# Keys' squares in rounded parts, summed by rounded matmuls, with the first query product ahead of the sums

## The chip, the cores and the metric

The kernel runs on one core of a Trainium2 chip. The metric is the device time of one execution in microseconds (us). The engines of the core work side by side, each through its own list of instructions in order, and meet at semaphores: PE (TensorE, matmuls), ACT (ScalarE), DVE (VectorE), POOL (GpSimd) and SP (which only issues transfers here).

## What is computed

Two layers of a decoder block on 528 tokens (16 meta tokens and 512 others), 1024 channels wide. Each layer normalizes its input, multiplies it by one wide matrix and feeds three mixers: a gated linear recurrence, a short gated convolution and an attention of 8 heads with low-rank queries and keys. The mixers' gated outputs are projected, merged and added back. The part that matters here is how the keys are normalized:

```python
def rms_norm(x, g):
    xf = x.astype(jnp.float32)
    y = xf * lax.rsqrt(jnp.mean(xf * xf, axis=-1, keepdims=True) + EPS)
    return (y * g.astype(jnp.float32)).astype(x.dtype)

def mla(...):
    q = (rms_norm(c_q, cq_g) @ w_uq).reshape(b_, t_, MLA_HEADS, QK_HEAD)
    ckv = rms_norm(c_kv, ckv_g)
    k_nope = (ckv @ w_uk).reshape(b_, t_, MLA_HEADS, QK_NOPE)
    v = (ckv @ w_uv).reshape(b_, t_, MLA_HEADS, V_HEAD)
    k_r = jnp.broadcast_to(k_rope[:, :, None, :], (b_, t_, MLA_HEADS, QK_ROPE))
    k = jnp.concatenate([k_nope, k_r], axis=-1)
    q = rms_norm(q, qn_g)
    k = rms_norm(k, kn_g)        # the sum of squares over a head's 192 channels
    ...
```

## The kernel before

Everything lies with channels on the 128 partitions and the 528 tokens along the free dimension. A product of two float32 matrices is made of three matmuls on rounded operands (type fp32r in the profile): each operand is split into an upper part, rounded to fp32r, and a lower part, the rest. Upper times upper, lower times upper and upper times lower are accumulated in PSUM (`product`, L499, its matmuls at L507). 528 columns make two matmuls of 264. POOL splits each 512 KB weight unit as it arrives (`split`, L411 to L420); ACT and DVE split activations: ACT writes the upper part, DVE subtracts it from the whole (`lo_part`, L1093).

Attention works through pairs of heads, four pairs in each of two layers, so eight turns of one loop (`Fori` over `PAIRS`; PE's loop starts at L647, ACT's at L878, DVE's at L1242, POOL's at L450). A turn on PE goes in this order: values for four token tiles (`va`, L660), keys of two heads (`kn0`, `kn1`, L507), values of the fifth token tile (`vb`, L660), the sums of the keys' squares (`sum_k0`, `sum_k1`, L557), the queries of two heads (`qn0`, `qn1`), their rotated part (`qr`), then "fill" steps. A fill step is six matmuls of an ordinary projection of the layer, which belongs to the convolution mixer and to the gates; its products have the names `c0`, `x0`, `g0`, `b0` and so on. Fill steps stand wherever PE would otherwise wait: five of them, then the queries' sums of squares by token (`stat_q`, L541, one column each, in three portions with a fill step behind each portion), 16 more, and then ten rounds of scores (L572, L575), fill, and transposes of the probabilities (L590). `b0` is the first fill product behind the first scores.

The sum of squares over the channels is a sum over partitions. `spread_sum` (L554) makes it with a matmul whose stationary operand is a 128x128 tile of ones, which leaves the sum in every partition. Squares and ones are float32 there, so this is a float32 matmul; the profile has two records for each one.

The other engines in a turn, in their orders. ACT: upper part of `va` (L883); for each key head its square (L888) and the key times its gain (L890), which frees the key's PSUM slot; upper part of `vb` (L893); two square roots (L897), which wait for DVE's sums; then square and upper part of each query (L903, L904) and of `qr` (L907, L909). DVE: lower part of `va` (L1245) and of `vb` (L1251), squares of keys plus the squares of the shared rotated part (L1258, twice), a reciprocal (L1264) and the lower part of a query (L1270) for each head, then the keys' normalization and lower parts and those of the rotated parts (L1279 to L1316), a small reciprocal (L1319), and the convolution's input (L1384), which frees the PSUM slot that `b0` takes. POOL: weight units, and between units 3 and 4 the addition of the queries' squares (L467), for which `stat_q` waits.

PSUM is used as four slots of two banks each. `TILES` (L80) lists which product takes which slot and which semaphore it signals; a product waits until the slot's last reader has let it go. Waits are counts computed from these tables.

Of the kernel before, what the change touches and what calls it, by code (L numbers as in the profile page):

```python
# [28 lines left out]
P = 128  # L29
# [56 lines left out]
            ("sum_k0", 0, "att_mm"), ("sum_k1", 1, "att_mm"), ("qn0", 2, "att_mm"), ("qn1", 3, "unit_used"),  # L86
# [9 lines left out]
for _s in ("MR", "MS"):  # L96
# [16 lines left out]
    "k_squared": ("ATT", 2), "v_hi": ("ATT", 2), "k_sum": ("ATT", 1), "k_rms": ("ATT", 2), "q_summed": ("ATT", 2), "k_rinv": ("ATT", 2), "k_full": ("ATT", 2), "kr_scaled": ("ATT", 2),  # L113
# [35 lines left out]
def build(nc, xt, w_units, w_pair, params, hparams, consts, rope, stream):  # L149
    with ExitStack() as ctx:  # L150
# [64 lines left out]
        ones = sb("ones", [P, P])  # L215
        lane_consts = sb("lane_consts", [P, 2 + 2 * NTOK])
# [179 lines left out]
        def _(pool):  # L396
            pool.memset(ones[:], 1.0).then_inc(sem("made"), 1)
            pool.memset(eps, EPS).then_inc(sem("made"), 1)
# [88 lines left out]
        def _(pe):  # L487
# [123 lines left out]
            for l in range(DEPTH):  # L611
# [33 lines left out]
                with nc.Fori(0, PAIRS, engines=bass.OrderedEngineSet([pe.engine]), head_slot={pe.engine: 0}) as p:  # L645
# [26 lines left out]
                    for h in range(2):  # L672
                        out = free("ATT", l, p, f"sum_k{h}")
                        pe.wait_ge(*at("k_squared", l, p, h + 1))
                        spread_sum(out, ct[h]).then_inc(sem("att_mm"), 1)

                    pe.wait_ge(*was_read("CQ", l, 0, "q2"))
                    hi, lo = unit_ready("ATT", l, p, 1)
                    for h in range(2):
                        out = free("ATT", l, p, f"qn{h}")  # L680
                        product(out, lambda k: hi(3 * h + k), lambda k: lo(3 * h + k), tiles(cq_hi), tiles(cq_lo),
                                KQ).then_inc(sem("unit_used" if h else "att_mm"), 1)
                    out = free("ATT", l, p, "qr")
# [91 lines left out]
        def _(act):  # L775
# [50 lines left out]
            for l in range(DEPTH):  # L826
# [51 lines left out]
                with act.Fori(0, PAIRS) as p:  # L878
# [7 lines left out]
                    for h in range(2):  # L886
                        act.wait_ge(*ready("ATT", l, p, f"kn{h}"))
                        act.activation(halves(ct[h][:]), slot(slot_of("ATT", f"kn{h}")), ACT.Square).then_inc(  # L888
                            sem("k_squared"), 1)
                        act.activation(halves(ct[2 + h][:]), slot(slot_of("ATT", f"kn{h}")), ACT.Identity, bias=zero,  # L890
                                       scale=hparam(l, KN_G)).then_inc(freed("ATT", f"kn{h}"), 1)
# [22 lines left out]
                    for h in range(2):  # L914
                        act.wait_ge(*at("k_full", l, p, h + 1))
                        act.activation(kn_hi[:, h, :], ct[2 + h][:], ACT.Copy).then_inc(sem("k_hi"), 1)
# [175 lines left out]
        def _(dve):  # L1092
# [39 lines left out]
            for l in range(DEPTH):  # L1132
# [109 lines left out]
                with dve.Fori(0, PAIRS) as p:  # L1242
# [10 lines left out]

                    for h in range(2):
# [402 lines left out]
```

## Time and profile before

| | us |
|---|---|
| runs of the kernel (three) | 1724.68, 1726.32, 6525.27 |
| median | 1726.32 |
| the profiled execution, device time | 1722.76 |
| its span in the trace | 1721.0 |
| PE busy | 1700.5 (99%) |
| POOL busy | 1204.6 (70%) |
| DVE busy | 887.7 (52%) |
| ACT busy | 485.6 (28%) |

Times in the trace are microseconds from the start of the span. A row of the timeline has start, duration, engine, line and operation, output and inputs, and how many instructions are merged in it (x2). A matmul's duration is from its start to its modelled end; the next one starts long before that end, so the cost of a matmul in a row of many is the distance between starts. Brackets at the end of a row give the idle time ahead of it and what ended it. In a table of windows each row has the stretch, its length, the busy time of PE, PEld, DVE, ACT and POOL with their instructions, then PEclk, the granted clock of TensorE (1.00 for full speed), the busy share of the DMA engines and GB/s.

### The profile page before, as it was taken

To read this page: it belongs to the slowest core of one execution; us is meant where nothing else is said; L and a number is where in the kernel's file an instruction comes from. 1 tells how busy PE (TensorE), PEld (TensorE's weight loads), DVE (VectorE), ACT (ScalarE), POOL (GpSimd) and SP (SyncE) were. 2 spreads that over 40 slices of the span, in tenths; PEclk is the share of its full clock that TensorE was granted. 3 is DMA by queue.
4 is the path that set the end of the run, shared out by engine and by line. 5 is a ranking of instruction groups with operands and counts; after the bars stand their busy time and mean duration, and the time that the engine had idled before them with its cause. 6 is when DMAs were issued, how large, how long until landed. Compare 5 with 4: busy or idle time off the path is not lost.

```text
span 1721.0 us, 32258 instructions
## 1 busy us (share of the span) xinstructions
PE 1700.5 (99%) x11956; PEld 1593.7 (93%) x11956; DVE 887.7 (52%) x1281; ACT 485.6 (28%) x867; POOL 1204.6 (70%) x1365
## 2 busy tenths in 40 slices
PE   7999999999999999999999999999999999999999
PEld 7999999999999999999999998989898888888887
DVE  7966658485545452212349657584856455322221
ACT  5523233342313331101134333333323223311110
POOL 7764748385688777777766748483857898777773
PEclk9999999999999999999999999999999999999999
DMA  4421212122222223222432312121222322322233
GB/s 159 138 97 62 92 60 92 66 85 86 93 91 90 88 104 118 85 93 90 160 118 75 109 56 98 60 92 66 92 86 88 108 85 85 136 97 97 87 122 112
DMA packets 49407, 164.21 MB, mean 95 GB/s; under 512 B 6048, under 2 KB 7456, under 8 KB 49056
## 3 DMA queue, kind: packets, MB, share of 16 engines
q1 hardware_dynamic: 41328, 146.56, 25.4%
q10 hardware_dynamic: 8032, 17.03, 3.0%
q8 instruction: 29, 0.48, 0.1%
q14 instruction: 18, 0.15, 0.0%
HBM read 152.21 MB, written 10.81 MB: 95 GB/s over the span
## 4 chain that ended last, share of the span: by engine, by line
PE 96%; POOL 1%; DVE 1%; DMA 1%; ACT 0%; issue 0%; ACTq 0%; POOLq 0%; DVEq 0%
PE slots L507 84%; PE slots L572 4%; PE slots L605 3%; PE slots L660 2%; POOL early L467 1%; PE slots L590 1%; PE slots L541 1%; PE slots L557 1%; DMA residual_or_merged<-xt 1%; DVE spare L1115 0%; ACT early L907 0%; PE slots L575 0%; DVE branch_lo L1106 0%; PE slots L550 0%; DVE cq_lo L1150 0%
## 5 line engine op out<-in xcount | busy, mean ns | idle before, releaser
L419 POOL TENSOR_TENSOR w_lo<-w_raw,w_hi 128x256 fp32r<-128x256 f32 x1004 | 839.6, 866 | 20.9
L414 POOL TENSOR_SCALAR w_hi<-w_raw 128x1024 fp32r<-128x1024 f32 x251 | 290.5, 1157 | 345.9 <-PE slots L507 337.1
L507 PE MATMUL slots<-h_hi,w_hi 128*128 128x264 f32 (+1 forms) x2112 | 523.5, 312 | 0.0
L507 PE MATMUL slots<-h_lo,w_hi 128*128 128x264 f32 (+1 forms) x2112 | 517.1, 309 | 0.0
L507 PE MATMUL slots<-h_hi,w_lo 128*128 128x264 f32 (+1 forms) x2112 | 515.9, 308 | 0.0
L507 PEld LDWEIGHTS slots<-h_hi,w_hi 128*128 128x128 f32 x2112 | 343.8, 189 | 19.3
L507 PEld LDWEIGHTS slots<-h_hi,w_lo 128*128 128x128 f32 x2112 | 343.1, 189 | 19.1
L507 PEld LDWEIGHTS slots<-h_lo,w_hi 128*128 128x128 f32 x2112 | 343.2, 189 | 17.8
L507 PE MATMUL slots<-branch_hi,w_hi 128*128 128x264 f32 (+1 forms) x576 | 143.7, 313 | 9.9 <-DVE branch_lo L1106 9.2
L507 PE MATMUL slots<-branch_lo,w_hi 128*128 128x264 f32 (+1 forms) x576 | 142.4, 311 | 0.0
L507 PE MATMUL slots<-branch_hi,w_lo 128*128 128x264 f32 (+1 forms) x576 | 142.0, 310 | 0.0
L1463 DVE SCALAR_TENSOR_TENSOR gated<-gate_tanh,slots 128x528 f32<-128x528 f32 (+1 forms) x32 | 22.3, 696 | 179.4 <-PE slots L507 179.4
L507 PEld LDWEIGHTS slots<-branch_hi,w_hi 128*128 128x128 f32 x576 | 94.6, 190 | 16.6 <-issue 10.6
L1017 ACT ACTIVATE gate_tanh<-slots,channel_params 128x528 f32<-128x528 f32 (+1 forms) x48 | 33.4, 695 | 269.1 <-PE slots L507 269.0
L507 PEld LDWEIGHTS slots<-branch_lo,w_hi 128*128 128x128 f32 x576 | 94.0, 189 | 5.6
L507 PEld LDWEIGHTS slots<-branch_hi,w_lo 128*128 128x128 f32 x576 | 94.0, 189 | 5.5
L952 ACT ACTIVATE residual_or_merged<-slots,r_bias,q_sc 106x106 f32<-106x106 f32 (+4 forms) x80 | 49.4, 617 | 165.1 <-DVE r_bias L1337 165.1
L1359 DVE TENSOR_TENSOR pt_lo<-slots,pt_hi 106x106 fp32r<-106x106 f32 (+4 forms) x80 | 37.0, 463 | 65.3 <-ACT pt_hi L965 38.9
L1094 DVE TENSOR_TENSOR branch_lo<-sc_back,branch_hi x16 | 17.4, 1124 | 92.0 <-ACT branch_hi L1074 92.0
L965 ACT ACTIVATE pt_hi<-slots 106x106 fp32r<-106x106 f32 (+1 forms) x64 | 25.1, 393 | 125.7 <-PE slots L590 125.7
L414 POOL TENSOR_SCALAR w_rope_hi<-w_rope_raw 128x384 fp32r<-128x384 f32 x8 | 4.1, 513 | 74.3 <-PE slots L605 74.3
L1264 DVE RECIPROCAL early<-early 128x528 f32<-128x528 f32 x16 | 55.2, 3448 | 1.0
(234 smaller groups left out, 2828.1 us busy)
## 6 DMA issues: line engine op xcount, KB each, us to landing
w_raw<-w_units SPq DMA_DIRECT2D x251, 512.0 KB, 3.3
stream<-sc_acc ACTq DMA_DIRECT2D x16, 264.0 KB, 2.1
sc_back<-stream SPq DMA_DIRECT2D x2, 2112.0 KB, 8.0
x_old<-stream SPq DMA_DIRECT2D x16, 264.0 KB, 4.6
stream<-residual_or_merged ACTq DMA_DIRECT2D x16, 264.0 KB, 2.5
ab_raw<-w_units SPq DMA_DIRECT2D x8, 512.0 KB, 4.3
residual_or_merged<-xt ACTq DMA_DIRECT2D x4, 528.0 KB, 7.9
stream<-xt ACTq DMA_DIRECT2D x1, 2112.0 KB, 11.7
```

Source lines behind the costliest of these rows:

```text
L414: pool.tensor_scalar(hi, raw, 1.0, 1.0, ALU.mult, ALU.mult).then_inc(sem("hi_part"), 1)
L419: op = pool.tensor_tensor(lo[:, cols], raw[:, cols], hi[:, cols].bitcast(F32), ALU.subtract)
L507: mm = pe.matmul(out[:, a_, 0:t1 - t0], w(k), x(k)[:, t0:t1], start=(n == 0), stop=(n == 3 * ks - 1))
L572: mm = pe.matmul(bank[:, 0:k1 - k0], q[:, q0:q0 + nq], k[:, k0:k1], start=(m == 0), stop=(m == 4 and not masked))
L605: mm = pe.matmul(out[:, a_, q0 - a_ * HALF:q1 - a_ * HALF], v[0:nk, j, h * VHEAD:(h + 1) * VHEAD], pt[0:nk, j * PT_STEP + q0:j * PT_STEP + ...
L660: mm = pe.matmul(out[0:nt_, t % 4 // 2, (t % 2) * 256:(t % 2) * 256 + 256], x[:, k, t0:t0 + nt_], w[0][:, cols], start=(k == 0 and n == 0) ...
L952: act.activation(dst, src, ACT.Exp, bias=r_bias[0:nq, n:n + 1], scale=q_sc[0:nq, n:n + 1], accum_out=r_sum[0:nq, n:n + 1]).then_inc(sem("p ...
L965: act.activation(dst[:, :, 0:nq], src[:, :, 0:nq], ACT.Copy).then_inc(sem("turned_hi"), 1)
L1017: act.activation(kept_halves(l, g_t[n][:]), kept_slot(l, n), ACT.Tanh, bias=param(l, which, i * 2 + n), scale=0.5).then_inc(freed(stage, f ...
L1264: dve.reciprocal(ct[4 + h][:], ct[4 + h][:]).then_inc(sem("k_rinv"), 1)
L1359: dve.tensor_tensor(lo[:, :, 0:nq], src[:, :, 0:nq], hi[:, :, 0:nq].bitcast(F32), ALU.subtract).then_inc(done, 1)
L1463: dve.scalar_tensor_tensor(out, kept_halves(l, g_t[n][:]), 1.0, kept_slot(l, 2 + n), ALU.add, ALU.mult).then_inc(freed(stage, f"{y}{n}"), 1)
```

## The change

The squares of each key head are now kept as two rounded parts. ACT computes the square twice, into float32 (`ct[h]`) and rounded into `kn_hi[:, h]`; DVE subtracts the second from the first into `kn_lo[:, h]`, by its `lo_part`. PE sums each head with four fp32r matmuls (two halves, each with the upper and the lower part) against a rounded tile of ones, `ones_r`, which POOL makes once at the start. `kn_hi` and `kn_lo` hold the normalized key later in the same turn; ACT's write of it waits for the second sum. The first query product `qn0` now stands ahead of the two sums.

```diff
-            ("sum_k0", 0, "att_mm"), ("sum_k1", 1, "att_mm"), ("qn0", 2, "att_mm"), ("qn1", 3, "unit_used"),
+            ("qn0", 2, "att_mm"), ("sum_k0", 0, "att_mm"), ("sum_k1", 1, "att_mm"), ("qn1", 3, "unit_used"),
...
+        ones_r = sb("ones_r", [P, P], F32R)
...
+            pool.wait_ge(sem("made"), 1)
+            pool.tensor_scalar(ones_r[:], ones[:], 1.0, 1.0, ALU.mult, ALU.mult).then_inc(sem("ones_rounded"), 1)
...
-                    for h in range(2):
-                        out = free("ATT", l, p, f"sum_k{h}")
-                        pe.wait_ge(*at("k_squared", l, p, h + 1))
-                        spread_sum(out, ct[h]).then_inc(sem("att_mm"), 1)
-
                     pe.wait_ge(*was_read("CQ", l, 0, "q2"))
                     hi, lo = unit_ready("ATT", l, p, 1)
-                    for h in range(2):
+
+                    def queries(h):
+
                         out = free("ATT", l, p, f"qn{h}")
                         product(out, lambda k: hi(3 * h + k), lambda k: lo(3 * h + k), tiles(cq_hi), tiles(cq_lo),
                                 KQ).then_inc(sem("unit_used" if h else "att_mm"), 1)
+
+                    queries(0)
+                    for h in range(2):
+                        out = free("ATT", l, p, f"sum_k{h}")
+                        pe.wait_ge(*at("k_sq_lo", l, p, h + 1))
+                        for a_ in range(2):
+                            cols = slice(a_ * HALF, (a_ + 1) * HALF)
+                            for n, squares in enumerate((kn_hi, kn_lo)):
+                                mm = pe.matmul(out[:, a_, 0:HALF], ones_r[:], squares[:, h, cols], start=(n == 0),
+                                               stop=(n == 1))
+                        mm.then_inc(sem("att_mm"), 1)
+                    queries(1)
...
+                        act.activation(halves(kn_hi[:, h, :]), slot(slot_of("ATT", f"kn{h}")), ACT.Square).then_inc(
+                            sem("k_sq_hi"), 1)
...
+                        if h == 0:
+                            act.wait_ge(*ready("ATT", l, p, "sum_k1"))
                         act.activation(kn_hi[:, h, :], ct[2 + h][:], ACT.Copy).then_inc(sem("k_hi"), 1)
...
+                    for h in range(2):
+                        dve.wait_ge(*at("k_squared", l, p, h + 1))
+                        dve.wait_ge(*at("k_sq_hi", l, p, h + 1))
+                        lo_part(kn_lo[:, h, :], ct[h][:], kn_hi[:, h, :], "k_sq_lo")
```

On PE, between the fifth token tile's values and the second query product, before (`cq_hi` and `cq_lo` are the latent queries; the first group of `cq` rows is `qn0`, the row that waits for `slot_free3` begins `qn1`):

```order
L660 MATMUL slots<-w_hi,kv_lo 104x256
L513 REGISTER_ALU
L674 REGISTER_ALU [waits slot_free0]
L557 MATMUL slots<-early,ones 128x264 [waits k_squared]
L557 MATMUL slots<-early,ones 128x264
L513 REGISTER_ALU
L674 REGISTER_ALU [waits slot_free1]
L557 MATMUL slots<-early,ones 128x264 [waits k_squared]
L557 MATMUL slots<-early,ones 128x264
L492 REGISTER_ALU [waits slot_free0]
L513 REGISTER_ALU [waits unit_split]
L507 MATMUL slots<-cq_hi,w_hi 128x264 [waits slot_free2]
```

And the same place now, from the last rows of `qn0` on:

```order
L510 MATMUL slots<-cq_hi,w_lo 128x264 x2
L516 REGISTER_ALU
L687 REGISTER_ALU [waits slot_free0]
L691 MATMUL slots<-kn_hi,ones_r 128x264 [waits k_sq_lo]
L691 MATMUL slots<-kn_lo,ones_r 128x264
L691 MATMUL slots<-kn_hi,ones_r 128x264
L691 MATMUL slots<-kn_lo,ones_r 128x264
L516 REGISTER_ALU
L687 REGISTER_ALU [waits slot_free1]
L691 MATMUL slots<-kn_hi,ones_r 128x264 [waits k_sq_lo]
...
L516 REGISTER_ALU
L510 MATMUL slots<-cq_hi,w_hi 128x264 [waits slot_free3]
```

The sums now stand between the two query products, with twice the matmuls, and wait for DVE (`k_sq_lo`) and no longer for ACT alone (`k_squared`).

On DVE, from the lower parts of the values to the first reciprocal, now (before, the row with `kn_lo` was not there and the rest was the same):

```order
L1261 TENSOR_TENSOR v_lo<-slots,v_hi 106x1024 [waits v_hi]
L1266 REGISTER_ALU
L1267 TENSOR_TENSOR v_lo<-slots,v_hi 104x256 [waits v_hi]
L1110 TENSOR_TENSOR kn_lo<-early,kn_hi 128x528 [waits k_sq_hi,k_squared] x2
L1275 ISA
L1278 TENSOR_TENSOR early<-slots,residual_or_merged 128x528 [waits slot_free3,att_mm]
L1275 REGISTER_ALU
L1278 TENSOR_TENSOR early<-slots,residual_or_merged 128x528 [waits att_mm]
L1284 RECIPROCAL early<-early 128x528 [waits k_rms]
```

The two subtractions stand behind the lower part of `vb`, which needs ACT's copy of it, and ahead of everything that DVE does with the sums.

## Rows read from the trace of the kernel before

**Rows 1.** The page: the span, and busy time of the engines.
```profile
span 1721.0 us, 32258 instructions
...
PE 1700.5 (99%) x11956; PEld 1593.7 (93%) x11956; DVE 887.7 (52%) x1281; ACT 485.6 (28%) x867; POOL 1204.6 (70%) x1365
```

**Rows 2.** PE's waits: who waited for whom, total us, times, longest.
```profile
PE slots L507 <- DVE branch_lo L1106: 9.2, 4, 8.6
PE slots L541 <- POOL early L467: 4.5, 8, 0.6
```

**Rows 3.** PE's timeline, third pair of layer 0: float32 sums, then queries.
```profile
253.17 2.06 PE L557 MATMUL slots<-early,ones 128*128 128x264 f32 x8
254.87 0.60 PE L507 MATMUL slots<-cq_hi,w_hi 128*128 128x264 f32 x2
255.31 0.41 PE L507 MATMUL slots<-cq_lo,w_hi 128*128 128x264 f32 x2
...
257.27 0.41 PE L507 MATMUL slots<-cq_hi,w_hi 128*128 128x264 f32 x2
```

**Rows 4.** ACT's timeline, same pair: squares, gained keys, `vb`, square roots.
```profile
251.20 0.61 ACT L888 ACTIVATE early<-slots 128x528 f32<-128x528 f32 x1 [0.35 <-PE slots L507]
251.71 0.79 ACT L890 ACTIVATE early<-slots,lane_consts,head_params 128x528 f32<-128x528 f32 x1
...
253.16 0.79 ACT L890 ACTIVATE early<-slots,lane_consts,head_params 128x528 f32<-128x528 f32 x1
253.84 0.38 ACT L893 ACTIVATE v_hi<-slots 104x256 fp32r<-104x256 f32 x1
255.33 1.42 ACT L897 ACTIVATE early<-early,lane_consts 128x528 f32<-128x528 f32 x2 [1.11 <-DVE early L1258]
```

**Rows 5.** DVE's timeline, same pair.
```profile
254.26 0.42 DVE L1251 TENSOR_TENSOR v_lo<-slots,v_hi 104x256 fp32r<-104x256 f32 x1 [2.15 <-ACT v_hi L893]
254.60 1.38 DVE L1258 TENSOR_TENSOR early<-slots,residual_or_merged 128x528 f32<-128x528 f32 x2
256.10 3.45 DVE L1264 RECIPROCAL early<-early 128x528 f32<-128x528 f32 x1
...
263.41 0.67 DVE L1270 SCALAR_TENSOR_TENSOR qn_lo<-slots,head_params,qn_hi 128x528 fp32r<-128x528 f32 x1
```

**Rows 6.** POOL's timeline: same pair, and the first pair of layer 0.
```profile
254.22 2.12 POOL L419 TENSOR_TENSOR w_lo<-w_raw,w_hi 128x256 fp32r<-128x256 f32 x3
...
67.84 1.06 POOL L414 TENSOR_SCALAR w_hi<-w_raw 128x1024 fp32r<-128x1024 f32 x1 [4.42 <-DMA w_raw<-w_units]
```

**Rows 7.** Instructions of `lo_part` on DVE: ns min/median/max, first and last start.
```profile
L1094 DVE TENSOR_TENSOR kn_lo<-early,kn_hi x16: 1235/1257/1276, 82.9 to 1226.5; 128x528 fp32r<-128x528 f32 x16
...
L1094 DVE TENSOR_TENSOR kv_lo<-early,kv_hi x4: 696/697/700, 51.1 to 917.8; 128x528 fp32r<-128x528 f32 x4
```

**Rows 8.** Same pair, the queries' sums: POOL's addition, then PE.
```profile
262.62 3.25 POOL L467 TENSOR_TENSOR early<-early 64x528 f32<-64x528 f32 x2 [5.59 <-ACT early L907]
...
265.05 0.40 PE L507 MATMUL slots<-h_hi,w_lo 128*128 128x264 f32 x2
266.02 0.88 PE L541 MATMUL slots<-ones,early 128*106 128x1 f32 x8 [0.56 <-POOL early L467]
```

**Rows 9.** `b0`: DVE's last release and PE's first `b0` matmul, layer 0, then layer 1.
```profile
280.59 0.71 DVE L1384 TENSOR_TENSOR sc_pad<-slots,sc_c 128x528 f32<-128x528 f32 x1 [0.22 <-DVE q_sc L1319]
...
282.44 0.47 PE L507 MATMUL slots<-h_hi,w_hi 128*128 128x264 f32 x2
...
1049.03 0.71 DVE L1384 TENSOR_TENSOR sc_pad<-slots,sc_c 128x528 f32<-128x528 f32 x1 [0.22 <-DVE q_sc L1319]
...
1050.57 0.45 PE L507 MATMUL slots<-h_hi,w_hi 128*128 128x512 f32 x1
```

**Rows 10.** Windows after `stat_q`, pairs two and three: busy us, PE first; granted clock third from last.
```profile
172.10:178.90 6.80, 6.80 (x34) 6.80 (x33) 6.70 (x11) 3.45 (x8) 6.72 (x6) 0.50 0.22 77
...
268.50:275.30 6.80, 6.80 (x59) 6.80 (x58) 6.70 (x11) 4.42 (x8) 6.72 (x6) 1.00 0.23 77
```

More of the change, by code:

```diff
@@ L112 @@
     "rope_split": ("ATT", 1), "att_mm": ("ATT", 10),
-    "k_squared": ("ATT", 2), "v_hi": ("ATT", 2), "k_sum": ("ATT", 1), "k_rms": ("ATT", 2), "q_summed": ("ATT", 2), "k_rinv": ("ATT", 2), "k_full": ("ATT", 2), "kr_scaled": ("ATT", 2),
+    "k_squared": ("ATT", 2), "k_sq_hi": ("ATT", 2), "k_sq_lo": ("ATT", 2), "v_hi": ("ATT", 2), "k_sum": ("ATT", 1), "k_rms": ("ATT", 2), "q_summed": ("ATT", 2), "k_rinv": ("ATT", 2), "k_full": ("ATT", 2), "kr_scaled": ("ATT", 2),
     "k_hi": ("ATT", 2), "k_lo": ("ATT", 2), "krp_hi": ("ATT", 2), "krp_lo": ("ATT", 2),
```

## The prediction

> **What bounds the kernel now.** I read the page first: PE is busy for 1700.5 of 1721.0 us [rows 1]. Then PE's waits: besides one wait of 8.6 us at the start the only one that comes back in every turn of the attention loop is that of `stat_q` for POOL, 8 times and 4.5 us in all [rows 2]. So PE sets the time; a matmul taken off it is worth its distance to the next start, and a wait put on it costs as long as it is. What decides here is how much air the other engines have behind PE in one stretch, from the keys to the first scores. For that I read the timelines of all engines in the third pair of layer 0 [rows 3 to 9]; the other pairs agree with it within some hundredths from one start to the next, the first pair of each layer aside, where DVE and ACT are later.
>
> **What the sums cost and will cost.** The four float32 matmuls (eight records) run from 253.17 to 254.87, 1.70 us, and the query behind them loses 0.19 more (254.87 to 255.31 for two matmuls, where two otherwise take 0.24) [rows 3]. fp32r matmuls of 264 columns stand (257.27 - 255.31)/16 = 0.122 us apart [rows 3], so eight take 0.98. The swap gives 1.89 - 0.98 = 0.91 us a turn, 7.3 us in eight turns. That is all there is to gain.
>
> **What the sums will wait for.** Times are those of the third pair [rows 3 to 5]. PE is through with `vb` at 253.17 and does `qn0` at once (its slot, that of `va`, is free by then): 18 x 0.122 = 2.20, to 255.37.
> - ACT does one more square for each key. A square costs 0.51 from start to start (251.20 to 251.71), a gained key 0.68 (253.16 to 253.84) [rows 4]. The row is now 251.20, 251.71, 252.22 for the first head, 252.90, 253.41, 253.92 for the second, and `vb` at 254.60 and not 253.84. It ends at 254.98.
> - DVE's lower part of `vb` starts at 255.02 and is through at 255.44; the next instruction may start 0.08 before that (254.26 + 0.42 against 254.60) [rows 5]. Then the two new subtractions. The trace has such instructions at two prices: 0.70 us where POOL rests (`kv_lo`) and 1.26 where POOL splits weights (`kn_lo`, same shape) [rows 7]. In this stretch POOL is splitting a unit until 256.34 at least [rows 6], and slowed by DVE it goes on longer. So I take the higher price: ends at 256.6 and 257.8. The lower one would give 256.1 and 256.7. In the first pair of layer 0 POOL waits for a transfer from 63.4 to 67.8 [rows 6], and the lower price holds.
> - A wait costs PE 0.15 from the release to the first matmul (265.87 to 266.02) [rows 8]. First sum from 256.75, 1.4 us after PE was free; second from 257.97, 0.7 us after the first; `qn1` from 258.46. Before it began at 257.27 [rows 3]. PE is 1.2 us late: the 0.9 gained is gone, and 2.1 of waiting came.
>
> The Trainium skill, page "SBUF — State Buffer", section "Who interferes with whom", speaks against the new work: a VectorE instruction with two inputs in SBUF contends with a GpSimd instruction that reads SBUF, and whichever is first keeps the shared ports to its end. By that rule each subtraction would wait for the rest of a POOL piece of 0.7 us (2.12 for three [rows 6]) and take 0.7 to 1.4, which puts the second one's end between 256.7 and 258.1; the trace agrees, with 1.26 against 0.70 [rows 7].
>
> **What is late next.** DVE adds the second sum once it has landed, at about 258.65 to 259.35; then the reciprocals (3.45) follow. The first was at 256.10, bound by ACT's root [rows 4, 5], and is now at 259.35 at the latest. This chain of reciprocal, query, reciprocal, query has no air in it (256.10 to 264.08), so all behind it on DVE shifts by D = 3.25; if the first subtraction has the ports partly for itself, D is 2.9. I take D = 3.1. In the first pair of layer 0, by the same steps with 0.70 for a subtraction, D = 2.3.
> - `stat_q` takes the slot of `qn1`, which DVE frees at the end of that chain: before at 264.08, two microseconds ahead of PE; now at 267.2, so PE starts at 267.3 and not 266.02 [rows 5, 8]. POOL's addition is no longer what ends the wait: ACT is at `qr` when PE delivers it, 1.2 late. So PE is 1.3 late here, of which 1.2 was already there.
> - All through the keys' normalization to L1384 DVE has no pause but one of 0.22, so its release of `b0`'s slot shifts by D too. Before it came at 281.30 and PE, adding 0.15, wanted it at 282.44: air of 0.99. In layer 1 (pieces of 512 columns, a quicker fill) it is 1050.57 - 0.15 - 1049.74 = 0.68 [rows 9]. So PE's delay at `b0` is D less the air: 2.1 us a turn in layer 0 and 2.4 in layer 1. The 1.3 from `stat_q` are within that, not on top.
> - Behind `b0` rounds of scores, softmax and transposes hang on PE's own start of the scores, so they shift as one.
>
> Other parts cost nothing: `ones_r` is made once at the start, where POOL goes on to wait for the first weights (if that cover were gone: one instruction of 128 columns, and L414 does 1024 in 1.06 us [rows 6], so 0.1 to 0.3 us with its wait); ACT's wait for the second sum lies a dozen microseconds before its write.
>
> **The sum.** First pair of layer 0: 2.3 - 0.99 = 1.3. Three further pairs of layer 0: 2.1 each, four of layer 1: 2.4 each. Together 1.3 + 6.3 + 9.6 = 17.2 us. The gain of 7.3 is already in it, since it is worked out from starts.
>
> **The clock.** In pair two of layer 0 the granted clock fell to 0.50 (1.2 GHz) right behind `stat_q` and stayed for 6.8 us. 34 matmuls ran in this window against 59 in the same stretch of the next pair [rows 10]: 6.8 x 25/59 = 2.9 us lost. It came after the wait of 0.56 and the matmuls of one column, and seven other pairs with the same rows kept 2.4 GHz. Now the wait there is about 1.0 us and a new one of 2.1 us in two pieces stands before. So I expect it in more pairs. Part of a loss at `stat_q` falls into the air that PE now has at `b0` (2.1 - 1.3 = 0.8 in layer 0, 1.1 in layer 1), so a fall costs about 2 there, and one at the sums next to nothing. Before had one at 2.9; I take one and a half to two of them now at 2, +3 to 4 against -2.9, in all 0.5 more. Bounds: none now, -3; one in each pair, 16 - 3 = +13.
>
> The profiled execution took 1722.76, so the sum is 1722.76 + 17.2 + 0.5 = 1740.5. The two undisturbed runs, 1724.68 and 1726.32, lie 2 to 3.5 above it, so a median should come out near **1742 us**, 0.9% slower.
>
> **Rivals.**
> - *The clock falls in most pairs.* Speaking for it: each turn has two stretches poorer in matmuls than the one that brought it down. Against: seven of eight kept the clock. 17 + 13 gives 1755. Chance 0.15.
> - *The shift is small.* The subtractions take 0.70 in each pair, D = 2.3 and delays of 1.3 and 1.6: 4 x 1.3 + 4 x 1.6 = 12, less the 2.9 if pair two keeps the clock, 9: 1734. For it: they start just as POOL ends a unit. Against: POOL still has two of four pieces to do. Chance 0.15.
> - *Faster: the sums find their parts ready.* One mechanism: `qn0`'s 2.2 us cover ACT's and DVE's new work. Then only the swap counts, 7.3 us, and 1718 comes out. It decides at one point: the second lower part must be there by 255.7, and by my steps it is 2 us later, since it queues behind `vb` on two engines. For it speaks only that POOL and PE stay as they are. Chance 0.07.
> - *The change does not do what it says,* the fp32r sums cost as much as float32 ones. The waits hide it: a second sum of 0.85 in place of 0.49 gives 0.4 more in D, 1745. Inside my range, not counted by itself.
>
> **Chances and range.** My forecast 0.63, the rivals 0.15, 0.15 and 0.07. The forecast's own range, from D between 2.9 and 3.25 and the clock between none and three falls, is 1736 to 1748. For eight in ten I leave the faster case out below and the last of the clock case above: 1729 to 1756. A measurement of this kernel can tell about 2%, 35 us, from no change. Faster by that would need five times what the swap gives: 0.01. Slower by that needs a fall of the clock in each pair and more: 0.05. Within 2%: 0.94.
>
> **What would show it.** In the changed profile: eight records of sums a turn 0.12 us apart within a head; PE waiting 1 to 1.5 us for DVE's `kn_lo` ahead of the first and 0.5 to 0.7 ahead of the second; `kn_lo` of squares at 1.2 us except in the first pair; `stat_q` released by DVE's L1290 in place of POOL; a wait ahead of the first scores or of `b0`, ended by DVE, summing to about 2 us a turn with that at `stat_q`; stretches of half clock in the attention pairs. I am wrong if PE shows no wait at the sums, if DVE's chain up to the scores is shorter than before, or if a wait stands in the score rounds.

## The result and the profile after

| | before | after |
|---|---|---|
| median, us | 1725.5 | 1743.45 |
| single runs, us | 1724.68, 1726.32, 1721.55, 6525.27 | 1744.5, 1743.41, 1742.77, 1743.5 |
| profiled execution, its span, us | 1722.76, 1721.0 | 1744.5, 1742.7 |
| mean granted clock of that span | 0.996 | 0.989 |

The ratio is 1.0116, with the interval 1.0103 to 1.013: the change costs 1.2%. The single run of 6525.27 is not among the fast runs that the ratio compares. In the experiments below, other runs of the kernel before on the chips used there had medians between 1723.01 and 1723.61.

The page of the changed kernel has these two rows, to set against [rows 1]:

```profile
span 1742.7 us, 32307 instructions
...
PE 1709.0 (98%) x11956; PEld 1602.6 (92%) x11956; DVE 896.2 (51%) x1297; ACT 491.5 (28%) x883; POOL 1213.8 (70%) x1366
```

With 16 new instructions each, DVE is busy 8.5 us longer, in an engine that is busy half of the time, and ACT 5.9. Neither is a load, yet PE now waits for them. These are PE's waits in the changed kernel (who waited for whom, us in all, times, longest), to set against [rows 2]:

```profile
PE slots L691 <- DVE kn_lo L1110: 7.9, 15, 0.8
PE slots L544 <- DVE qn_lo L1290: 5.6, 8, 0.9
PE slots L510 <- issue: 3.7, 1, 3.7
```

The sums wait for `kn_lo` (15 of 16 sums), and `stat_q` waits for DVE in all eight turns, where it had waited for POOL. This is the third pair of layer 0, all engines, some rows left out, to set against [rows 3 to 5]. The turn starts at 252.31; before's started at 246.65, so 5.66 is to be taken off for a comparison.

```profile
256.85 0.61 ACT L900 ACTIVATE early<-slots 128x528 f32<-128x528 f32 x1 [0.35 <-PE slots L510]
...
259.02 0.63 ACT L902 ACTIVATE kn_hi<-slots 128x528 fp32r<-128x528 f32 x1
259.51 0.82 ACT L904 ACTIVATE early<-slots,lane_consts,head_params 128x528 f32<-128x528 f32 x1
259.87 3.74 POOL L422 TENSOR_TENSOR w_lo<-w_raw,w_hi 128x256 fp32r<-128x256 f32 x4
260.18 0.42 ACT L907 ACTIVATE v_hi<-slots 104x256 fp32r<-104x256 f32 x1
260.63 0.42 DVE L1267 TENSOR_TENSOR v_lo<-slots,v_hi 104x256 fp32r<-104x256 f32 x1 [2.88 <-ACT v_hi L907]
260.98 2.04 DVE L1110 TENSOR_TENSOR kn_lo<-early,kn_hi 128x528 fp32r<-128x528 f32 x2
261.92 0.39 PE L691 MATMUL slots<-kn_hi,ones_r 128*128 128x264 f32 x1 [0.74 <-DVE kn_lo L1110]
262.14 0.28 PE L691 MATMUL slots<-kn_lo,ones_r 128*128 128x264 f32 x1
262.27 0.28 PE L691 MATMUL slots<-kn_hi,ones_r 128*128 128x264 f32 x1
262.39 0.28 PE L691 MATMUL slots<-kn_lo,ones_r 128*128 128x264 f32 x1
...
263.07 0.39 PE L691 MATMUL slots<-kn_hi,ones_r 128*128 128x264 f32 x1 [0.40 <-DVE kn_lo L1110]
...
263.87 0.71 DVE L1278 TENSOR_TENSOR early<-slots,residual_or_merged 128x528 f32<-128x528 f32 x1 [0.24 <-PE slots L691]
264.49 3.44 DVE L1284 RECIPROCAL early<-early 128x528 f32<-128x528 f32 x1
...
272.52 0.91 PE L544 MATMUL slots<-ones,early 128*106 128x1 f32 x8 [0.66 <-DVE qn_lo L1290]
```

It reads downward as one queue. ACT reaches `vb` only at 260.18, DVE's lower part of it comes at 260.63, and behind that stand the two subtractions, ending at 263.02. PE has finished `qn0` at 261.0 and waits twice. The reciprocals begin at 264.49, which is 258.83 in before's times, against 256.10 [rows 5]: 2.7 us late. Everything that DVE does up to the convolution's input inherits that.

**Where 21.7 us of span went.** Turns are measured from their own start to `b0`, in us:

| turn | before | after | difference |
|---|---|---|---|
| start of the program to the first turn | 55.29 | 59.27 | +4.0 |
| first pair of layer 0 | 37.34 | 40.61, clock fell | +3.3 |
| second | 38.85, clock fell | 37.26 | -1.6 |
| third | 35.79 | 37.23 | +1.4 |
| fourth | 35.79 | 39.75, clock fell | +4.0 |
| first pair of layer 1 | 37.07 | 41.07, clock fell | +4.0 |
| second, third | 35.50 | 37.26 | +1.8 each |
| fourth | 35.50 | 39.47, clock fell | +4.0 |

That adds up to 22.6 before rounding; 0.9 is regained in the rest of the layers. (In both traces the clock also stood at 0.50 for 3.4 us around the start of the first turn of each layer, from 56.0 and 923.0 before and from 58.8 and 932.6 after. As both kernels have these two, they are not among the falls counted here.) A turn in which the clock stayed costs 1.45 (layer 0) or 1.76 (layer 1); one in which it fell costs some 2.2 to 2.5 more (39.75 against 37.23, 39.47 against 37.26). The windows of the changed kernel, to set against [rows 10] (busy us of PE, PEld, DVE, ACT and POOL with their instructions, then granted clock, DMA share, GB/s), show these four falls and, last, the same stretch of a turn without one:

```profile
82.70:89.50 6.80, 6.80 (x34) 6.80 (x34) 6.66 (x10) 3.27 (x6) 6.72 (x7) 0.50 0.24 77
369.40:376.20 6.80, 6.80 (x34) 6.80 (x34) 6.66 (x11) 2.74 (x5) 6.72 (x6) 0.50 0.23 77
956.50:963.30 6.80, 6.80 (x33) 6.80 (x33) 6.66 (x11) 2.96 (x5) 6.72 (x7) 0.50 0.23 77
1239.80:1246.60 6.80, 6.80 (x34) 6.80 (x33) 6.66 (x10) 3.19 (x6) 6.72 (x7) 0.50 0.24 77
272.60:279.40 6.80, 6.80 (x61) 6.80 (x62) 6.73 (x6) 2.97 (x5) 6.63 (x7) 1.00 0.09 22
```

So the 21.7 are three things: about 12.3 in the turns without the clock, 9.4 for four falls less 3.1 for the one that before had, and 4.0 at the start of the program, less the 0.9. The 9.4 is an estimate, four times the mean of 2.52 and 2.21, since the two first pairs have no turn without a fall beside them in this trace; the 12.3 is what it leaves. The 4.0 at the start I had put at nothing.

### The profile page after: what moved, and what is told of

The parts are those of the page before. It is cut to its first block, busy times and chain, and to the rows that moved or that the text cites. A ratio compares the mean times of both kernels' runs of the same rounds, so it can differ in the third digit from the quotient of the medians.

```text
span 1742.7 us, 32307 instructions
## 1 busy us (share of the span) xinstructions
PE 1709.0 (98%) x11956; PEld 1602.6 (92%) x11956; DVE 896.2 (51%) x1297; ACT 491.5 (28%) x883; POOL 1213.8 (70%) x1366
## 4 chain that ended last, share of the span: by engine, by line
PE 89%; POOL 4%; DVE 3%; issue 2%; ACT 1%; DMA 0%; POOLq 0%; DVEq 0%
PE slots L510 79%; PE slots L575 3%; POOL w_lo L422 3%; PE slots L608 3%; DVE early L1284 2%; PE slots L663 2%; PE slots L593 1%; POOL w_hi L417 1%; DVE kn_lo L1110 1%; PE slots L544 1%; POOL early L470 1%; ACT early L904 1%; PE slots L691 0%; DMA w_raw<-w_units 0%; ACT kn_hi L902 0%
## 5 line engine op out<-in xcount | busy, mean ns | idle before, releaser
L422 POOL TENSOR_TENSOR w_lo<-w_raw,w_hi 128x256 fp32r<-128x256 f32 x1004 | 851.0, 877 | 20.9
```

Of the source, the lines that this page charges most:

```text
L422: op = pool.tensor_tensor(lo[:, cols], raw[:, cols], hi[:, cols].bitcast(F32), ALU.subtract)
```

## Experiments

The theory: DVE's chain, from the subtractions over reciprocals and normalization to the release for `b0`, decides, and half clock behind `stat_q` and the start come on top. Rivals: the order of the products or the kind of the matmuls is itself to blame. All ratios are to the kernel before in runs of the same group on the same chip.

**1. The start.** The tile of ones is rounded behind the last of POOL's small start-up writes, and PE waits for it before the first turn.

```diff
-            pool.wait_ge(sem("made"), 1)
-            pool.tensor_scalar(ones_r[:], ones[:], 1.0, 1.0, ALU.mult, ALU.mult).then_inc(sem("ones_rounded"), 1)
             pool.memset(eps, EPS).then_inc(sem("made"), 1)
...
             pool.memset(token[:, 12:13], 0.0).then_inc(sem("sc_stored"), 16)
+            pool.wait_ge(sem("made"), 1)
+            pool.tensor_scalar(ones_r[:], ones[:], 1.0, 1.0, ALU.mult, ALU.mult).then_inc(sem("ones_rounded"), 1)
...
+                    pe.wait_ge(sem("ones_rounded"), 1)
```

> The changed kernel, with the rounded tile of ones made by POOL behind its start-up signals instead of ahead of them, and one wait of PE for it. In the trace of the changed kernel SP's first load is issued at 1.58 us and not 1.19, lands 2.2 us later than before, and PE then idles 3.7 us ahead of its second unit; the query sums of the first stage come 4.0 us later (28.82 against 24.78). Theory 1: POOL's extra instruction holds back the first weights behind the inputs and costs these 4 us: about 1739 to 1740 us, first load back at 1.2 us. Theory 2: the start varies by itself from kernel to kernel: no change, 1743.

Measured: 1741.25 (1734.19 to 1742.57), ratio 1.011 (1.009 to 1.013), 2.2 us below the changed kernel, which is at the edge of what these runs can tell. The trace tells more. In the changed kernel POOL's start-up and SP's first weight load stand so:

```profile
1.04 0.30 POOL L400 TENSOR_SCALAR ones_r<-ones 128x128 fp32r<-128x128 f32 x1
...
1.58 0.41 SPq L336 DMA_DIRECT2D w_raw<-w_units  x1
...
7.72 0.40 POOL L442 TENSOR_SCALAR w_hi<-w_raw 128x256 fp32r<-128x256 f32 x1 [5.81 <-DMA w_raw<-w_units]
```

In the kernel before SP issues that load at 1.19 and POOL has the weights at 5.53:

```profile
1.19 0.41 SPq L335 DMA_DIRECT2D w_raw<-w_units  x1
...
5.53 0.40 POOL L439 TENSOR_SCALAR w_hi<-w_raw 128x256 fp32r<-128x256 f32 x1 [4.00 <-DMA w_raw<-w_units]
```

One instruction of 0.30 us, with its wait, delays the load by 0.39, the weights by 2.19, and PE's first one-column product from 24.78 to 28.82. In the experiment the load is back at 1.19 and that product at 25.22. Over all traces taken, the three with the early rounding have it at 28.15 to 28.82, the others at 24.78 to 26.87. So the start costs 1.3 to 4 us. How the 0.39 grows no run here separates, and the first weights' arrival alone does not carry it: in the third of these traces, experiment 4's changed kernel, POOL has the weights at 6.32, as early as in the kernels without the early rounding (5.53 to 6.73), and the product still comes at 28.15. What all three share is the second load, landed at 9.55 to 9.67 where the others have it at 7.47 to 8.54.

The four runs also price the clock: one at a mean granted clock of 0.995 took 1734.19, with a single fall behind `stat_q` (79.1, first pair; one of 6.8 us from 925.6 begins ahead of the first turn of layer 1), the other three at 0.989 to 0.990 took 1741.2 to 1742.6.

**2. One part of the change alone.** First the order alone: before's float32 sums, with `qn0` ahead of them.

```diff
-            ("sum_k0", 0, "att_mm"), ("sum_k1", 1, "att_mm"), ("qn0", 2, "att_mm"), ("qn1", 3, "unit_used"),
+            ("qn0", 2, "att_mm"), ("sum_k0", 0, "att_mm"), ("sum_k1", 1, "att_mm"), ("qn1", 3, "unit_used"),
```

> The kernel before, with only the order changed: first query product ahead of the two float32 sums. By my theory (DVE's chain from the second sum to the release for b0 is what counts) the second sum lands 2.2 us later than before, D is about 1.5 to 2.2, less the air of 0.99 and 0.68 gives 0.5 to 1.5 us a turn: 1730 to 1736, with no wait at the sums. The rival, that only waits of PE at the sums cost, expects no change from before, 1725.

Then the swap of kinds alone, in before's order, with the late tile of ones and without the lower parts: ACT writes the square once, rounded, and four fp32r matmuls a head read it. This kernel leaves out the lower part and counts the upper one twice, so its sums are not those of the change; only its time is of use.

```diff
-                        act.activation(halves(ct[h][:]), slot(slot_of("ATT", f"kn{h}")), ACT.Square).then_inc(
+                        act.activation(halves(kn_hi[:, h, :]), slot(slot_of("ATT", f"kn{h}")), ACT.Square).then_inc(
...
-                        spread_sum(out, ct[h]).then_inc(sem("att_mm"), 1)
+                        for a_ in range(2):
+                            cols = slice(a_ * HALF, (a_ + 1) * HALF)
+                            for n in range(2):
+                                mm = pe.matmul(out[:, a_, 0:HALF], ones_r[:], kn_hi[:, h, cols], start=(n == 0),
+                                               stop=(n == 1))
...
```

> The kernel before, in its own order, with the sums made by eight fp32r matmuls a turn. ACT writes the square once, rounded, and the matmuls read this upper part twice, so the lower part is left out and the sum is doubled: the result is not the reference's. It has the matmuls of the change without its new work on ACT and DVE. Theory: the swap alone gives 0.9 us a turn, 7.3 in all: 1718. Rival: the air in front of stat_q is gone, since POOL's addition then ends the wait; it moves along with the query products, so no loss; if it did not, 1723 to 1725.

Measured: order alone 1733.18 (1731.76 to 1734.68), ratio 1.0064 (1.0043 to 1.0084), +10.2 us. Swap alone 1715.16 (1714.11 to 1716.51), ratio 0.9955 (0.9943 to 0.9968), -7.8 us. PE's waits for the order alone:

```profile
PE slots L541 <- DVE qn_lo L1274: 5.4, 8, 0.7
```

and PE's timeline for the swap alone, third pair of layer 0:

```profile
250.49 0.65 PE L682 MATMUL slots<-kn_hi,ones_r 128*128 128x264 f32 x4
251.40 0.75 PE L682 MATMUL slots<-kn_hi,ones_r 128*128 128x264 f32 x4 [0.26 <-ACT early L899]
```

With the order alone no sum waits, but the sums come later to DVE: its second `qn_lo` ends 19.30 after the turn's start and not 17.43, `stat_q` waits for it, and `b0` comes at 36.37 and 36.40, +0.6 and +0.9 a turn; two turns had a fall of the clock behind `stat_q` (`b0` at 38.57). The new order has a price of its own besides. `qn0` takes the slot of `va`, and in the first pair of layer 1 DVE frees it too late for a `qn0` that now comes ahead of the sums:

```profile
929.65 0.54 PE L507 MATMUL slots<-cq_hi,w_hi 128*128 128x264 f32 x2 [1.92 <-DVE v_lo L1249]
```

There the clock fell for 3.4 us as well, and `b0` came at 40.13, against 37.07 in before: 3.1 of the 10.2 us lie in this one turn. A late sum costs through DVE's chain although PE waits for nothing at the sum. With the swap alone DVE's chain stands where it stood (17.43), `stat_q` comes 0.95 earlier, no clock falls behind it, and `b0` comes at 35.01 and 35.02, now held by DVE's release. The swap does what it is meant to do; what the change adds around it takes more than that.

**3. The subtractions' place.** As experiment 1, and DVE does the two subtractions ahead of the lower part of `vb`.

```diff
+                    for h in range(2):
+                        dve.wait_ge(*at("k_squared", l, p, h + 1))
+                        dve.wait_ge(*at("k_sq_hi", l, p, h + 1))
+                        lo_part(kn_lo[:, h, :], ct[h][:], kn_hi[:, h, :], "k_sq_lo")
                     nl = TOKS[4][1]
...
-                    for h in range(2):
-                        dve.wait_ge(*at("k_squared", l, p, h + 1))
-                        dve.wait_ge(*at("k_sq_hi", l, p, h + 1))
-                        lo_part(kn_lo[:, h, :], ct[h][:], kn_hi[:, h, :], "k_sq_lo")
```

> The changed kernel with the late tile of ones and, on DVE, the two subtractions of the squares ahead of the lower part of vb, so that they don't queue behind ACT's copy of it. Theory: the first subtraction starts at 5.7 us of a turn, the second ends at about 8.3, inside the first query product, so PE waits for neither; D falls from 2.75 to about 1.5, the delay at b0 to 0.3 (layer 0) and 0.6 (layer 1): 1728 to 1731, above before, since the chain on DVE is longer still. Rival (PE's waits at the sums are the loss): with these gone the gain of 7.3 shows: 1718 to 1720.

Measured: 1730.26 (1728.06 to 1738.34), ratio 1.005 (1.003 to 1.007), 11 us below experiment 1. DVE's timeline there, third pair of layer 0, whose turn starts at 251.59:

```profile
257.35 1.29 DVE L1111 TENSOR_TENSOR kn_lo<-early,kn_hi 128x528 fp32r<-128x528 f32 x1 [0.31 <-ACT kn_hi L903]
...
259.04 1.07 DVE L1111 TENSOR_TENSOR kn_lo<-early,kn_hi 128x528 fp32r<-128x528 f32 x1 [0.39 <-ACT kn_hi L903]
```

and PE's waits there, where no row of a sum is left:

```profile
PE slots L544 <- DVE qn_lo L1291: 8.7, 8, 1.1
```

Both lower parts are there before PE has finished `qn0`; the chain is 1.46 late and not 2.75, and `b0` comes at 35.55 where the clock stays (two turns of layer 1). About eleven of the changed kernel's 18 us above before hang on DVE's queue order alone. What is left is `stat_q`, for which PE, no longer held at the sums, waits 1.1 each time; in the profiled execution (the slowest, 1738.34) the clock fell there in five turns, for 6.8 to 10.2 us each.

**4. The clock, by moving two fill steps.** Seven fill steps stand ahead of `stat_q` and 14 behind it, in place of five and 16, so that the same work fills the wait. The changed kernel was run unchanged beside it, then the same edit in before and in experiment 3's kernel.

```diff
-FILLS = (5, 16, 4, 4, 4, 5, 5, 2, 6, 6, 7, 7, 6)
+FILLS = (7, 14, 4, 4, 4, 5, 5, 2, 6, 6, 7, 7, 6)
```

> The changed kernel once more, beside the next three on the same chip. Two things are open from its first trace. The start: its query sums of the first stage came at 28.82 us, against 24.78 in the kernel before and 25.2 to 26.9 in three kernels that make the rounded ones late or not at all. If POOL's extra instruction ahead of the start-up signals is the cause, 28 us or more comes again; if it is chance, something between 24.8 and 27. The clock: four pairs with a stretch of half clock in the first trace, granted clock of 0.990 in all runs; the same again, about 1743 us.

> The changed kernel with two of the fill steps moved from behind stat_q to ahead of it (seven and fourteen in place of five and sixteen); nothing else. DVE's chain to b0 stays as it is, 37.26 us into a turn. Theory: PE no longer waits at stat_q (0.7 to 0.9 us a turn now), but waits the longer at the scores or at b0, so the wait as such gives nothing; what goes is the poor stretch in which the clock fell in four pairs, at 2.2 to 3.4 us each: 1733 to 1737, granted clock 0.994 or more. Rival, that the falls come from the wait at the sums: the clock stays at 0.990 and the time at 1743.

> The kernel before with the same two fill steps moved. Here there is air at b0 (0.99 and 0.68 us), so taking away the wait of 0.56 at stat_q should give its whole length, 4.5 us in all, and the clock's fall in one or two pairs (2.9 us) goes too: 1716 to 1719. Rival: POOL or DVE becomes late in its place and nothing is gained: 1723.

> The changed kernel with the late tile of ones, the two subtractions ahead of the lower part of vb, and the two fill steps moved. With the subtractions early it ran 1730 and its DVE chain let b0 go at 35.5 us of a turn, like before; the profiled one had five pairs with half clock. Theory: without the wait at stat_q these go, b0 stays at 35.5 (37.6 in the first pair of a layer): 1719 to 1723, the first form of the change that is no slower than the kernel before. Rival (the clock falls for the waits at the scores): 1728 to 1730 again.

| kernel | median (lowest to highest) | ratio | clock of its runs |
|---|---|---|---|
| changed, again | 1744.52 (1742.39 to 1746.23) | 1.0117 (1.0098 to 1.0136) | 0.988 to 0.990 |
| changed, fill moved | 1734.21 (1732.56 to 1740.46) | 1.0069 (1.0042 to 1.0095) | 0.994 to 0.997 |
| before, fill moved | 1715.21 (1714.37 to 1716.29) | 0.9947 (0.993 to 0.9964) | 0.997 to 0.999 |
| experiment 3, fill moved | 1720.22 (1718.36 to 1722.62) | 0.9978 (0.9968 to 0.9989) | 0.996 to 0.999 |

The unchanged repeat had its four falls in the same four turns, within 0.3 us of the same places (82.4, 369.1, 956.2, 1239.5). With the fill moved the profiled executions of all three had none behind `stat_q`. PE's timeline of the changed kernel with the fill moved:

```profile
269.76 0.41 PE L510 MATMUL slots<-h_hi,w_lo 128*128 128x264 f32 x2
270.00 0.82 PE L544 MATMUL slots<-ones,early 128*106 128x1 f32 x8
```

its window behind `stat_q`:

```profile
270.00:276.80 6.80, 6.80 (x62) 6.80 (x61) 6.63 (x7) 2.85 (x5) 6.68 (x6) 1.00 0.16 50
```

and what PE waits for there:

```profile
PE slots L691 <- DVE kn_lo L1110: 7.8, 14, 0.8
PE slots L575 <- DVE qr_hi_and_lo L1110: 7.1, 8, 1.1
```

The `stat_q` wait is gone, and half clock with it. But `b0` still comes at 37.23: the wait has gone on to the first scores (L575), since DVE's chain ends when it ended. So only the clock's part could be had by refilling, about 10 us; the chain's part could not. Before gains 8.4 in the same way: there POOL's wait held `stat_q` and DVE had air, so `b0` itself comes at 35.03 and 34.81, 0.7 earlier, besides one fall less. Without falls behind `stat_q` on either side the change costs 1734.21 - 1715.21 = 19 us, of which 1.4 are at the start by these two traces (first turn at 58.64 against 57.25; 2.2 by experiment 1's times). With the subtractions first it still costs 1720.22 - 1715.21 = 5.0 us: `b0` at 35.55 against 35.03 and 34.81. The changed kernel and experiment 3's came as expected, before 0.8 us below its range.

Before with the fill moved has the lowest ratio of this study: 0.53% faster than before.

**5. Is the release of `b0` the last limit?** If so, an earlier one should bring the swap's whole gain home. DVE does the convolution's input ahead of `qr`'s lower part, and two fill steps of the score rounds go ahead of `stat_q`; experiment 3's kernel and before's, both with that.

```diff
-FILLS = (5, 16, 4, 4, 4, 5, 5, 2, 6, 6, 7, 7, 6)
+FILLS = (7, 16, 4, 4, 4, 5, 4, 1, 6, 6, 7, 7, 6)
...
+                    sc_input(0)
                     for h in range(2):
...
-                    sc_input(0)
                     for n in range(10):
```

> The changed kernel with the late tile of ones, the subtractions ahead of the lower part of vb, and room for DVE's chain: seven fill steps ahead of stat_q, sixteen behind (two more than before in all, taken back in the sixth and seventh round), and DVE's release of b0's slot two instructions earlier, so that PE can begin b0 ahead of the first scores. Theory: what holds the change back is only DVE's chain against PE's place at scores and b0. With 1.46 us more of PE's work ahead of the scores no wait is left in a turn, and the swap's 0.9 us a turn shows: against 1715.2 of the kernel before with the two fill steps moved, 7 us less, 1708 to 1711, faster than both kernels. Rival: the chain is late all the same, or a round is too short of cover: 1715 or more.

> The kernel before with the same room: fill steps and b0's release as in the other one, float32 sums in their old place. In it only 0.1 to 0.3 us a turn was left to gain after the two fill steps were moved, so 1714 to 1716; the distance to the other kernel, 5 to 7 us, is then what the swap is worth once its waits are covered. Rival: the swap is worth nothing by itself, and both come out alike.

Measured: 1730.03 (1728.73 to 1731.13), ratio 1.0035 (1.0019 to 1.0051), and 1732.54 (1732.38 to 1734.99), 1.0051 (1.0036 to 1.0065). Both miss what was expected by 16 us or more. The fills were two steps further on in the rounds, and there PE met another release of DVE; PE's waits of the first of the two:

```profile
PE slots L510 <- DVE sc_gate L1426: 10.6, 8, 1.4
```

A second pair of kernels takes the two steps from the end of the last round. It also does DVE's `sc_gate` and ACT's copy earlier, and the second half of the convolution a round later (of the edit only the first part is shown):

```diff
-FILLS = (5, 16, 4, 4, 4, 5, 5, 2, 6, 6, 7, 7, 6)
+FILLS = (7, 16, 4, 4, 4, 5, 5, 2, 6, 6, 7, 7, 4)
...
```

> The last two kernels took their two extra fill steps out of the sixth and seventh round and put the product ga0 ahead of DVE's release of its slot: PE waited 1.3 to 1.6 us a turn there (10.6 us in all) and some 0.5 us more in the shortened rounds. Now the two steps are taken from the very end of a turn, DVE frees ga0's slot in the first round, and ACT frees the second x product's slot ahead of the sixth softmax. Theory: with these two waits gone the swap's gain shows at last: 1708 to 1712, below both kernels and below the 1715.2 of the kernel before with two fill steps moved. Rival: the rounds have no air for any shift, a wait of the same size turns up in another one: 1718 or more.

> The kernel before with the same orders of fill and releases, float32 sums in their place. Theory: no wait of size is left, 1714 to 1717, and the distance to the other kernel is the swap's 7 us, less 1 to 2 for the first pairs of the layers. Rival: both alike, then the swap is worth nothing even with its waits covered.

Measured: 1721.48 (1720.2 to 1722.35), ratio 0.9994 (0.9985 to 1.0002), and 1725.21 (1723.14 to 1726.72), 1.001 (1.0002 to 1.0019). Both miss again, by 8 us or more, and the first comes out where its rival put it (1718 or more). PE's waits of the first:

```profile
PE slots L510 <- ACT sc_c L937: 7.3, 8, 0.9
```

Again a new one a turn, now ACT's. The rounds have no air either: each move of two fill steps found another release late by about a microsecond. What these two pairs show beside that is that the swap, together with the new order and its subtractions placed first, was worth 2.5 and 3.7 us where another wait than DVE's chain decided. So the question that this experiment put is not answered, and whether all 7.3 can be had in one kernel with both parts kept stays open. No run has both rounded parts in before's order, either: what the new order buys the change is not shown.

## Why the prediction was right, and where its steps were wrong

The time came out at 1743.45 against 1742, inside even the narrow range. It did so with three terms of the sum wrong, two one way and one the other, and that is luck. Against the profiled execution the turns were 4.9 too high, the clock 5.8 and the start 4.0 too low, and 0.9 was regained: 4.0 in all, 1744.5 against the 1740.5 of the sum. Of these 4.0 the step from the profiled execution to a median took off 2.5: the forecast went up by 1.5 there, since before's profiled execution lay below two of its runs, and the changed kernel's, its slowest run, lay 1.05 above its median. The mechanism of the main term held: DVE's longer chain, less the air at `b0`.

- *The swap's gain, 0.91 us a turn:* right. The fp32r sums stand 0.12 us apart within a head, the first of each aside (0.22), and the swap alone gave 7.8 us against 7.3. The agreement is partly luck: `b0` came 0.8 and 0.5 earlier, 5 us in all, and about the rest is the clock, which did not fall behind `stat_q`.
- *The waits at the sums:* right in kind and cause (DVE behind `vb` behind ACT), less in size. By starts PE lost 0.9 us (261.01 to 261.92) and 0.6 (262.51 to 263.07) where 1.4 and 0.7 were forecast. The step "So I take the higher price: ends at 256.6 and 257.8" failed by half: the subtractions took 0.90 and 1.23, not 1.26 twice (0.70 in the first pair, as said), and ended at 256.2 and 257.4 in before's times. "Its slot, that of `va`, is free by then" failed in one turn: in the first pair of layer 1 PE waited 0.38 for it (1.92 with the order alone).
- *D = 3.1:* it was 2.75 (second `qn_lo` 20.17 after the turn's start against 17.43), for that reason alone. In the first pair 2.0 against 2.3.
- *`stat_q` 1.3 late, held by DVE and no longer by POOL:* kind right, and 0.86 measured (20.23 against 19.37), since D was smaller.
- *"All through the keys' normalization to L1384 DVE has no pause but one of 0.22, so its release of `b0`'s slot shifts by D too":* off by 0.27. From L1279 to L1319 DVE took 16.15 us before and 15.88 after; its instructions fell differently against POOL's. The release shifted by 2.45, and less the air of 0.99 and 0.68 that makes 1.46 and 1.77: measured 1.45 and 1.76. The air was read rightly. The profile puts what idle time is left ahead of `b0` down to a weight piece of POOL (L422, 1.2 us in four turns) and not to DVE, as I had said; by the times DVE fits: its L1404 starts at 288.69 and takes 0.71, and with 0.15 more PE starts `b0` at 289.54.
- *The turns together, 17.2:* about 12.3, by the two points above (0.6 a turn in eight turns) for the most. The sum also gave the first pair of layer 1 the full 2.4, though it names the first pair of each layer as different.
- *The clock, +0.5:* the term that was mis-sized most. Four falls came, not one and a half to two, and each cost 2.2 to 2.5 where two turns allow the comparison: +6.3 in place of 0.5. The rival "the clock falls in most pairs" had half of this right and the turns too high. "Seven of eight kept the clock" was no measure: with the idle time at `stat_q` up from 0.56 [rows 8] to 0.66 to 0.68 in seven of the turns, four did. Of these seven turns three fell and four did not. Over the kernels the count goes with the mean wait for DVE there: two falls at 0.7 (order alone), four at 0.7 (changed kernel, twice), one at 0.75 (experiment 1), five at 1.1 (experiment 3); that is a loose tendency and no rule. A fall at the sums "costs next to nothing" was never put to the proof, as none came there.
- *"`ones_r` is made once at the start, where POOL goes on to wait for the first weights", at nothing:* wrong. The work was hidden on POOL, but what stands behind it is the signal on which SP sends the first load, and that is not. 4.0 in this trace, 1.3 to 4 over all.
- *The rivals.* That the sums find their parts ready was wrong here, but experiment 3 made it true by order alone; even so DVE's chain left only 35.55 at `b0`. A shift as small as the second rival's (delays of 1.3 and 1.6) is close to what came, 1.45 and 1.76, and its 1734 is what the changed kernel takes with the clock falls taken away (1734.21).

Of what was named as a sign of error, nothing appeared: PE waits at the sums, DVE's chain is longer, and no wait stands in the score rounds. Two of the signs for it came smaller: 0.9 us ahead of the first sum for 1 to 1.5, and, with `b0`, 1.45 and 1.76 a turn by starts for about 2, of which the profile books 0.66 at `stat_q` and 0.30 at `b0` as idle.

On contention, the rows first: in the pair shown DVE's two subtractions took 0.90 and 1.23 while POOL split weights, against 0.70 with POOL at rest [rows 7], and POOL's four pieces took 3.74 in place of four times 0.71 [rows 6]. The rule of the Trainium skill, page "SBUF — State Buffer", section "Who interferes with whom", that whichever of the two is first keeps the shared ports to its end, agrees in kind: both engines lost time. The first pair of layer 1 in experiment 1 shows it most plainly. There two subtractions fell within one of POOL's pieces. They took 0.70 each, and the piece took 2.02 in place of 0.74, longer by 1.28 beside their 1.31:

```profile
937.72 2.02 POOL L422 TENSOR_TENSOR w_lo<-w_raw,w_hi 128x256 fp32r<-128x256 f32 x1
937.82 1.31 DVE L1111 TENSOR_TENSOR kn_lo<-early,kn_hi 128x528 fp32r<-128x528 f32 x2
```

One engine stood still while the other worked, as the rule has it. Which was first the rows do not show: POOL's piece has the earlier start by 0.10, and it was the one that stood still. So a subtraction pays between nothing and 0.6 beside a busy POOL (0.70 against 1.29 in experiment 3). That this goes by how they fall against its pieces is my reading; no run moved them for that alone.

## What to carry to other kernels

Ask of a cheaper matmul who has to prepare its operands and what stands behind that work in the preparing engine's queue: 0.9 us saved a turn on PE was paid for with 2.75 us on DVE's serial chain, of which only the air at its next release was free. Put such preparation ahead of what nobody waits for, and put independent matmuls where PE waits directly ahead of one-column ones; two moved fill steps were worth more here (8.4 us) than the swap by itself (7.8), and the swap with all its parts lost time beside before with the same fill, except in experiment 5. An instruction in a start-up sequence is not free because its engine idles next: look at who waits for the signal behind it.

## What the runs showed of the hardware

- A first weight load issued 0.39 us later went with PE's first one-column product 1.3 to 4 us later, over three traces against eleven. Its own arrival was 2.19 later in the changed kernel's trace and 0.79 in that with the fill moved.
- Half clock repeats within 0.3 us: a wait of 0.7 us (0.9 in the first pair), then one-column matmuls, then 6.8 us at 0.50 in the same four turns of both profiled executions of the changed kernel. The waits of 0.9 and 0.6 at the sums, followed by 264-column matmuls, brought no fall in any trace here; one of 1.92 ahead of such matmuls was followed by 3.4 us at 0.50 (order alone, from 930.0). Back at `stat_q`, why four of the eight turns and not the others stays open.
- The same subtraction took 0.70 with POOL at rest and 0.70, 0.90, 1.07, 1.23 and 1.29 us with POOL at work; where two of 0.70 lay within one instruction of POOL (experiment 1), that one took 2.02 in place of 0.74.
